# One encoder block on one core: late tokens' output projections on whole units, and expert-row fetches placed by when their slots come free

## The chip, the cores and the metric

The kernel runs on one core of a Trainium2 chip. The core has five engines with queues of their own: PE (TensorE, with its weight loads as PEld), DVE (VectorE), ACT (ScalarE), POOL (GpSimd) and SP (SyncE, which here only issues DMAs), and 16 DMA engines. The metric is the device time of one execution in microseconds. Before the change three runs took 2066.88, 2083.95 and 2086.36 us, so the median is 2083.95.

## The reference

One layer over 512 tokens of 1024 features, in fp32:

```python
h = rms_norm(x)
aq, ak, av, rq, rk, rv, rg, ga, gr = split(h @ w_in)
y_att = sliding_window_gqa(aq, ak, av, sinks) @ w_o_att      # 8 heads, 2 kv heads, own and previous chunk of 64
y_ret = (silu(rg) * group_norm(retention(rq, rk, rv))) @ w_o_ret   # 4 heads, keys of 256, values of 512
x = x + (sigmoid(ga) * y_att + sigmoid(gr) * y_ret) @ w_out
x = x + peer(rms_norm(x))     # 8 heads; top 16 of 128 x 128 experts by two half keys; gelu(h . down) * gate * up
x = x + sigmoid(rms_norm(x) @ w_ple_gate) * (p @ w_ple_proj)
out = rms_norm(x)
```

## The kernel before, in words

**Tokens.** The first 128 tokens (the early tile) go through the mixers first, up to their top-k lists; then the other 384 (the late tokens) follow. What is asked here is the late part.

**Weights.** All weights come as units of 128 x 1024 fp32, 512 KB each, through a ring of 8 slots `raw` that SP fills in the order of `late_units()` (line 73). A slot is loaded again once PE has used the unit 8 before (`wait_used`, for value and gate batches after the whole batch of four). In the late part a product with weights is made of three fp32r products: ACT makes the high half of a unit (`upper`, L700), POOL the low half (`lower`, L650), and PE runs hi x hi, hi x lo and lo x hi (`mm3`, L1184 to L1186) in `columns` (L1198; a key is one tile of 128 outputs) and `tokens` (L1214; four units together, tokens as outputs). The input is split too, for the norm and also for `b_hi`, `b_lo` (the gated retention outputs, `transposed_upper` on ACT and `transposed_lower` on DVE, L2080, and the attention outputs, L949 and L2174) and for the merged mixer output (`merged_lower`, L2205). ACT makes high halves up to four units ahead of the output that it next works on (`run_ahead`).

**Order in the late part.** For each retention head i: rq (2 units), rk (2), rv (4), `wor` of the head before (4 units, 8 keys), rg (4); group norm of the head at its end. Then ak, av, gr, `wor` of the last head, more gr; eight aq and four filler units, in whose loop attention is staged over DVE, ACT and PE (scores of head h in iteration h+2, transposes in h+3, values, `att_out` L1510, in h+4); then `woa` with ga between; `out`; 16 pq units with the norm; then 128 `dn` (expert down) and 128 `up` units. Of the down units every other one is split (even ones), the odd ones are multiplied whole with `h_whole`, which POOL makes at L673 when it reaches the first.

**Expert rows of the early tile.** The first tile's 128 experts per token are fetched one row per token at a time: POOL issues an indirect DMA of 128 x 1024 fp32 (512 KB) into one of 8 slots (`fetch`, L653 to L664), and DVE uses it (`row`, L1757; L1772 for down, L1780 for up). Rows 0 to 127 are of the early tile's down weights, 128 to 255 of its up weights, 256 to 383 the last tile's down weights, the rest its up weights, in the up stage. `ROWS_AFTER`, `AQ_ROWS`, `LIST_ROWS`, `SUM_ROWS` and `QUAD_ROWS` say between which of DVE's other work its rows stand; `FETCH` says behind which unit in POOL's order a fetch stands. A fetch of row r waits for row r-8 to be used. POOL works strictly in this order: for each unit its low half, if it has one, then its fetches.

**The lists.** From pq on DVE makes the top-k lists of the late tokens (`best`, 16 lists, with sums of pairs behind each odd one), five rows beside each: one row after each of its five steps. ACT copies key scores into 12 buffers; the copies of 12 to 15 wait for lists 0 to 3 (`s12_free`, L986), and the high half of unit 252 (`run_ahead(DN0 + LEAD - 1)`, L1008) stands behind the copy of key scores 14, which waits for list 2. The first gelu of the down stage stands behind the copy of 15. Units are numbered over all: pq is 232 to 247, dn begins at 248, up at 376. After 70 down units PE waits for the selected keys, which DVE gives after all lists.

## Time and profile before

| | before |
|---|---|
| runs | 2066.88, 2083.95, 2086.36 us |
| profiled execution | 2086.6 us, its span 2084.8 us |
| mean granted PE clock | 0.957 |
| busy in the span | PE 91%, PEld 72%, DVE 60%, ACT 27%, POOL 47% |
| chain that ended last | PE 55%, DVE 14%, DMA 12%, POOL 10%, issue 5%, ACT 3% |
| moved by DMA | 622.96 MB, mean 299 GB/s |

The share of an engine is its busy time over the span. The chain is followed back from the last instruction, at each step to what released it. An engine's timeline lists its instructions with, in brackets, the idle time before one and who ended it. Stages lie one after the other in time: early tile to 268 us, retention to 682, attention to 811, woa and out to 912, pq and lists to 1244, gates and down units to 1568, up units to 2011, the rest to the end.

### The profile page before, as it was taken

The numbers are of one execution on the slowest core, as the hardware profiler recorded it, in microseconds if no ns is written. First come the engines' busy times: TensorE is split into PE (matmuls) and PEld (weight loads), VectorE is DVE, ScalarE is ACT, GpSimd is POOL, SyncE is SP. The second block draws the span as 40 slices with busy tenths as digits, with TensorE's granted clock in tenths as the row PEclk, the third lists the DMA queues.
The fourth block names the chain that finished last, engine by engine and source line by source line (L and its number), as shares of the span: only waits on it lengthen the run. The fifth ranks groups of instructions, "written<-read, shape, count | busy, mean of one in ns | idle before, by whom it ended". The sixth has DMA issues, their size and how long they took to land.

```text
span 2084.8 us, 25711 instructions
## 1 busy us (share of the span) xinstructions
PE 1886.8 (91%) x9521; PEld 1503.3 (72%) x9521; DVE 1247.7 (60%) x2421; ACT 553.4 (27%) x1024; POOL 971.3 (47%) x726
## 2 busy tenths in 40 slices
PE   7999999989898669989899979999639999999998
PEld 7499987877778558989899878889634444444467
DVE  3120366756557664678779997775664455444556
ACT  1120132322233234333222227774100000000043
POOL 0000066676768426758876635456662222233222
PEclk9999999999999889999999989999868999999999
DMA  8777736777787545779999968999999999999941
GB/s 318 283 264 288 257 122 223 257 253 259 247 309 265 174 160 177 259 241 333 354 414 395 347 199 291 380 378 399 410 404 362 389 390 391 393 392 391 397 147 41
DMA packets 211687, 622.96 MB, mean 299 GB/s; under 512 B 19456, under 2 KB 60544, under 8 KB 210432
## 3 DMA queue, kind: packets, MB, share of 16 engines
q1 hardware_dynamic: 77392, 274.06, 35.5%
q0 software_dynamic: 73728, 268.47, 34.8%
q10 hardware_dynamic: 60464, 79.11, 11.1%
q8 instruction: 58, 0.95, 0.2%
q14 instruction: 45, 0.37, 0.1%
HBM read 580.67 MB, written 37.75 MB: 297 GB/s over the span
## 4 chain that ended last, share of the span: by engine, by line
PE 55%; DVE 14%; DMA 12%; POOL 10%; issue 5%; ACT 3%; SPq 0%; ACTq 0%; POOLq 0%; DVEq 0%
PE bank L1672 21%; DMA slots<-peer_down,scr 8%; PE bank L1184 6%; PE bank L1186 6%; PE bank L1185 6%; PE bank L1269 6%; POOL w_lo L650 5%; POOL slots L664 5%; DVE slots L1772 2%; PE bank L1290 2%; PE bank L1600 2%; DVE bank L1780 2%; DMA raw<-weights 2%; DMA slots<-peer_up,scr 1%; PE bank L1344 1%
## 5 line engine op out<-in xcount | busy, mean ns | idle before, releaser
L650 POOL TENSOR_TENSOR w_lo<-raw,w_hi 128x1024 fp32r<-128x1024 f32 x198 | 472.3, 2392 | 637.9 <-ACT w_hi L700 635.8
L1184 PE MATMUL bank<-hb,w_hi 128*128 128x384 f32 (+2 forms) x1320 | 450.2, 341 | 55.0 <-POOL w_lo L650 28.0
L1672 PE MATMUL bank<-raw,scr 128*128 128x512 f32 x1024 | 442.6, 595 | 28.1 <-DVE scr L2378 28.1
L1185 PE MATMUL bank<-hb,w_hi 128*128 128x384 f32 (+2 forms) x1320 | 431.5, 327 | 0.0
L1186 PE MATMUL bank<-hb,w_lo 128*128 128x384 f32 (+2 forms) x1320 | 431.2, 327 | 0.0
L1772 DVE SCALAR_TENSOR_TENSOR slots<-slots,bank 128x1024 f32<-128x1024 f32 x256 | 308.8, 1218 | 173.0 <-DMA slots<-peer_down,scr 165.4
L664 POOL DMA_INDIRECT slots<-peer_up,scr x256 | 244.2, 954 | 343.8 <-DVE bank L1780 291.6
L1672 PEld LDWEIGHTS bank<-raw,scr 128*128 128x128 f32 x1024 | 195.6, 191 | 274.7 <-issue 274.7
L700 ACT ACTIVATE w_hi<-raw 128x1024 fp32r<-128x1024 f32 x198 | 205.3, 1053 | 559.1 <-DMA raw<-weights 548.8
L1780 DVE SCALAR_TENSOR_TENSOR bank<-slots,scr,bank 128x1024 f32<-128x1024 f32 x254 | 325.7, 1282 | 33.7 <-DMA slots<-peer_up,scr 29.6
L1184 PEld LDWEIGHTS bank<-hb,w_hi 128*128 128x128 f32 x1320 | 262.4, 199 | 66.1 <-POOL w_lo L650 29.5
L664 POOL DMA_INDIRECT slots<-peer_down,scr x256 | 243.3, 950 | 108.4 <-issue 79.7
L1185 PEld LDWEIGHTS bank<-hb,w_hi 128*128 128x128 f32 x1320 | 262.4, 199 | 4.8 <-issue 1.0
L1186 PEld LDWEIGHTS bank<-hb,w_lo 128*128 128x128 f32 x1320 | 261.4, 198 | 2.9
L1600 PE MATMUL bank<-x_all,raw 128*128 128x256 f32 x1024 | 235.4, 380 | 1.0 <-ACT scr L1021 1.0
L1600 PEld LDWEIGHTS bank<-x_all,raw 128*128 128x128 f32 x1024 | 189.7, 191 | 24.0 <-issue 1.2
L2378 DVE TENSOR_TENSOR scr<-scr 128x256 f32<-128x256 f32 x128 | 54.7, 429 | 221.0 <-PE bank L1672 218.2
L1021 ACT ACTIVATE scr<-bank 128x256 f32<-128x256 f32 x128 | 48.4, 379 | 231.1 <-PE bank L1186 136.8
L1184 PE MATMUL bank<-w_hi,hb 128*128 128x512 f32 (+1 forms) x216 | 86.0, 398 | 19.3 <-POOL w_lo L650 15.7
L1269 PE MATMUL bank<-slots,raw 128*128 128x128 f32 x672 | 78.8, 279 | 10.8 <-DVE slots L1851 10.8
L1046 ACT ACTIVATE scr<-hb,scr 128x128 f32<-128x128 f32 x256 | 81.2, 391 | 23.2 <-DVE hb L2352 22.8
L1269 PEld LDWEIGHTS bank<-slots,raw 128*128 128x128 f32 x672 | 78.1, 196 | 11.8 <-issue 11.7
(304 smaller groups left out, 1861.6 us busy)
## 6 DMA issues: line engine op xcount, KB each, us to landing
raw<-weights SPq DMA_DIRECT2D x514, 512.0 KB, 6.7
act_scratch<-scr ACTq DMA_DIRECT2D x64, 256.0 KB
gate_scratch<-scr ACTq DMA_DIRECT2D x8, 2048.0 KB, 8.8
scr<-gate_scratch ACTq DMA_DIRECT2D x32, 512.0 KB, 16.5
scr<-act_scratch ACTq DMA_DIRECT2D x32, 512.0 KB, 20.5
slots<-peer_down,scr POOLq DMA_INDIRECT x256, 7.9
slots<-peer_up,scr POOLq DMA_INDIRECT x256, 7.9
x_all<-x_scratch ACTq DMA_DIRECT2D x1, 2048.0 KB, 17.4
```

Source lines behind the costliest of these rows:

```text
L650: nc.gpsimd.tensor_tensor(w_lo[:, s, :], raw[:, s, :], w_hi[:, s, :].bitcast(F32), ALU.subtract).then_inc(lo_done, 1)
L664: pool.indirect_dma_start(slots[:, r % R_SLOTS, :], None, up_d if part % 2 else down_d, bass.IndirectOffsetOnAxis(ap=ids[:, n:n + 1], axis ...
L700: nc.scalar.activation(w_hi[:, u_mod, :], raw[:, u_mod, :], ACT.Copy).then_inc(hi_done, 1)
L1046: ins = nc.scalar.activation(gated[q % 4][:, x, :], onehot(q, x, 1).bitcast(F32), ACT.Copy, scale=gates_s[:, t + x:t + x + 1])
L1184: nc.tensor.matmul(out, a_hi, c_hi, start=first, stop=False)
L1185: nc.tensor.matmul(out, a_hi, c_lo, start=False, stop=False)
L1186: return nc.tensor.matmul(out, a_lo, c_hi, start=False, stop=last)
L1269: ins = nc.tensor.matmul(out, raw[:, u % RING, k * P:k * P + P], rhs[:, k, :], start=k == 0, stop=k == KT - 1)
L1600: ins = nc.tensor.matmul(bank[:, c % 2, 0:T], raw[:, s, P * k:P * k + P], h_whole[:, k, :], start=k == 0, stop=k == KT - 1)
L1672: ins = nc.tensor.matmul(bank[:, b, :], wgt[:, c % 4, a], raw[:, s, 512 * n:512 * n + 512], start=first, stop=last)
L1772: ins = stt(out=u, in0=u, scalar=1.0, in1=row_bank, op0=ALU.mult, op1=ALU.mult, accum_out=dots[:, n:n + 1])
L1780: ins = stt(out=row_bank, in0=u, scalar=a, in1=row_bank, op0=ALU.mult, op1=ALU.add)
```

## The change

Part one: the 32 `wor`, `woa` and `out` units of the late tokens are no longer split. PE multiplies the raw unit with the unsplit input in plain fp32 (`whole_columns`), one product for three. So their high and low halves go, and with them the splits of the inputs: `transposed_lower`, the b_lo of attention and `merged_lower` on DVE, the copies of the merged output on ACT; ACT writes the unsplit inputs into `yT` and `att`, and `out` reads `yacc`.

Part two: in the attention loop the scaling of the probabilities (3 instructions a head) goes from DVE to ACT, behind ACT's copy of the transposes. The gelu of the early tile's dots goes from the attention loop to behind ga 4.

Part three: rows in the late mixers are spread otherwise. In the attention loop 20 rows in 7 iterations (3 each, the last 2) become 11 rows in 11; the 3, 6, 3 and 6 rows at the values and gates of heads 2 and 3 become 3, 4, 4 and 4, the 3, 3, 0 and 6 of head 1 become 3, 3, 3 and 4; woa 0 to 5 have 4 for 3; all in all 167 for 168 before the lists, and 89 for 88 in them. 66 rows stay behind the gates in both.

Part four: `FETCH` comes from a plan (`fetch_plan`) that steps through DVE's, PE's and POOL's work with costs in microseconds and puts each fetch behind the last unit whose low half begins before the slot comes free. From the code before and after, these are the numbers of fetches placed behind a unit, and in all up to it:

| units | before | after |
|---|---|---|
| 140, 141, 142 (head 1's values but the last) | 2, 4, 0 | 0, 0, 2 |
| 156, 157, 158 (head 2's) | 2, 2, 2 | 1, 1, 9 |
| 172, 173, 174 (head 3's) | 2, 2, 2 | 7, 0, 4 |
| 164, 165, 166 (gates of head 2's turn) | 2, 2, 2 | 2, 2, 2 |
| 180, 181, 182 (gates of head 3's turn) | 2, 2, 2 | 6, 3, 1 |
| up to 240 (pq 8) | 172 | 174 |
| up to 245 (pq 13) | 186 | 182 |
| up to 248 (dn 0) | 192 | 182 |
| up to 249 (dn 1) | 194 | 190 |
| up to 253 (dn 5) | 201 | 197 |
| up to 258 (dn 10) | 208 | 197 |
| up to 259 (dn 11) | 209 | 205 |
| up to 268 (dn 20) | 220 | 211 |
| up to 269 (dn 21) | 221 | 219 |
| up to 278, 279 (dn 30, 31) | 232, 233 | 225, 229 |
| up to 374 (dn 126), and at 375 | 371, 13 more | 354, 30 more |

The diff, cut to its core:

```diff
+def is_split(u):
+
+    return u >= NE and UNITS[u][0] not in ("wor", "woa", "out", "up") and (u < DN0 or u >= PP0 or (u - DN0) % 2 == 0)
+
+
+SPLITS = list(itertools.accumulate(int(is_split(_u)) for _u in range(NU)))
...
+    return SPLITS[u]
...
-ROWS_AFTER = {("rg", 0, LT - 1): 2,
-              ("rv", 1, 0): 3, ("rv", 1, 2): 3, ("rg", 1, LT - 1): 6}
+ROWS_AFTER = {("rg", 0, LT - 1): 2}
 for _i in range(1, RH):
-    for _k in (("rq", 2 * _i), ("rq", 2 * _i + 1), ("rk", 2 * _i), ("rk", 2 * _i + 1)):
-        ROWS_AFTER[_k] = 1
+    for _k, _n in ((("rq", 2 * _i), 1), (("rq", 2 * _i + 1), 1), (("rk", 2 * _i), 1), (("rk", 2 * _i + 1), 1 + (_i > 1)),
+                   (("rv", _i, 0), 3), (("rv", _i, 2), 3 + (_i > 1)), (("rg", _i, 0), 3 + (_i > 1)), (("rg", _i, LT - 1), 4)):
+        ROWS_AFTER[_k] = _n
     for _m in range(KT):
         ROWS_AFTER[("wor", _i - 1, _m)] = 1
-    if _i > 1:
-        ROWS_AFTER[("rv", _i, 0)], ROWS_AFTER[("rv", _i, 2)] = 3, 6
-        ROWS_AFTER[("rg", _i, 0)], ROWS_AFTER[("rg", _i, LT - 1)] = 3, 6
 for _k in (("ak", 0), ("ak", 1), ("gr", 0)):
-    ROWS_AFTER[_k] = 2
+    ROWS_AFTER[_k] = 3
 for _m in range(KT):
     ROWS_AFTER[("wor", RH - 1, _m)] = 1
+for _m in range(2, KT - 2):
+    ROWS_AFTER[("gr", _m)] = 2
 for _m in range(KT):
-    ROWS_AFTER[("woa", _m)] = 3 if _m + 2 < KT else 1
+    ROWS_AFTER[("woa", _m)] = 4 if _m + 2 < KT else 2
     ROWS_AFTER[("out", _m)] = 1 + _m % 2
 for _m in range(RAW_Q):
     ROWS_AFTER[("pq", _m)] = 2
-for _m in range(2, KT - 2):
-    ROWS_AFTER[("gr", _m)] = 2
-_left = NPAIR - sum(ROWS_AFTER.get(_k, 0) for _k in OUT if OUT[_k] < OUT[("aq", 0)])
-AQ_ROWS = {_i: min(3, max(0, _left - 3 * (_i - 1))) for _i in range(1, AH)}
-assert sum(AQ_ROWS.values()) == _left, _left
+AQ_ROWS = {_i: 1 for _i in range(1, AH + 4)}
+_n = sum(ROWS_AFTER.get(_k, 0) for _k in OUT if OUT[_k] < OUT[("woa", 0)]) + sum(AQ_ROWS.values())
+assert _n <= NPAIR, _n
+GELU_AT = next(_m for _m in range(KT) if _n + sum(ROWS_AFTER[("woa", _x)] for _x in range(_m + 1)) >= NPAIR)
...
+COST = {"wor": 5.3, "woa": 5.3, "out": 5.3, "aq": 6.8, "dn": 3.9}
+DVE_COST = {"rq": 1.2, "rk": 2.3, "wor": 0.6, "ak": 2.4, "gr": 0.8, "aq": 5.6, "woa": 1.2, "out": 2.2, "pq": 0.8}
+POOL_COST, FETCH_COST, ROW_COST, LANDING, SEARCH = 2.42, 1.07, 1.31, 8.0, 10.3
+DONE_AT = dict(zip(range(NE, UP0), itertools.accumulate(COST.get(UNITS[_u][0], 4.2) for _u in range(NE, UP0))))
...
+def row_events():
     for k in OUT:
+        if k == ("pq", RAW_Q):
+            break
+        u, less, extra = LAST_UNIT[k], 0.0, 0.0
         if k[0] in ("rv", "rg"):
+            less = 4.2 * 4 * (LT - 1 - k[2]) / LT
+        elif k[0] == "wor":
+            less = 2.6 * (1 - k[2] % 2)
+        if k[0] == "rv":
+            u, less = UNIT[("rk", 2 * k[1] + 1)], 0.0
+            extra = 25.0 if k == ("rv", 1, LT - 1) else 0.0
+        elif k[0] == "rg":
+            extra = (12.0 if k[1] == 1 else 3.0) if k[2] == 0 else 6.0 if k[2] == LT - 1 else 0.0
+        if k in FILLERS or k[0] == "aq":
+            yield u, less, 5.6, AQ_ROWS.get(k[1] if k[0] == "aq" else AH + FILLERS.index(k), 0), u + 3
+        elif k[0] == "rg" and k[2] == LT - 1:
+            yield u, less, 0.0, ROWS_AFTER.get(k, 0), u
+            yield u, 0.0, extra, 0, u
+        else:
+            yield u, less, DVE_COST.get(k[0], 0.0) + extra, ROWS_AFTER.get(k, 0), u + 3
+    last = UNIT[("pq", RAW_Q - 1)]
     for m in range(2 * PH):
+        yield last, 0.0, SEARCH, LIST_ROWS[m] + SUM_ROWS[m], last + 6 + 4 * m if m < 4 else DN0 + STEP * FIRST_Z + LEAD
+    at = DN0 + STEP * FIRST_Z
+    yield at, 0.0, 2.0, DOTS_EXP, at + LEAD + 4
+    yield at + SELECT_AT, 0.0, 2.0, DOTS_SELECT, at + LEAD + 6
     for j, quads in enumerate(QUAD_ROWS):
+        for q in range(4 * STEP // 2):
+            u = at + STEP * (j + 1) + q // 2
+            yield u, 0.0, 1.25, quads.count(q), u + 3
+    yield UP0 - 1, 999.0, 0.0, NLAST, UP0 - 1
...
+def fetch_plan():
+    used, fetch, pool, unit, at, behind = [], {}, 0.0, NE, 0.0, NE
+    first = DONE_AT[UNIT[("rg", 1)]]
+    for u, less, cost, rows, by in row_events():
+        at = max(at, DONE_AT[u] - less) + cost
+        for _ in range(rows):
+            free = max(first, used[-R_SLOTS] + ROW_COST + 0.5) if len(used) >= R_SLOTS else first
+            while unit < UP0:
+                ready = DONE_AT.get(unit - RING, 0.0) + 9.0 if unit < DN0 else DONE_AT[unit - LEAD] + 1.2
+                if is_split(unit):
+                    if max(pool, ready) >= free:
+                        break
+                    pool = max(pool, ready) + POOL_COST
+                unit += 1
+            pool = max(pool, free) + FETCH_COST
+            behind = max(behind, min(unit - 1, by, UP0 - 1))
+            fetch.setdefault(behind, []).append(len(used))
+            at = max(at, pool + LANDING)
+            used.append(at)
+            at += ROW_COST
+    assert len(used) == 3 * NPAIR, len(used)
+    return fetch
+FETCH = fetch_plan()
...
-ROW_USED, NLAST = row_uses()
-FETCH_LAG, FETCH_FIRST = 7, UNIT[("rg", 0)] + 6
-FETCH = {}
-_at = FETCH_FIRST
-for _r in range(3 * NPAIR):
-    if _r >= R_SLOTS:
-        _at = max(_at, ROW_USED[_r - R_SLOTS] + FETCH_LAG)
-    while len(FETCH.get(_at, ())) >= (2 if _r < R_SLOTS else 4):
-        _at += 1
-    FETCH.setdefault(min(_at, UP0 - 1), []).append(_r)
...
+        yT, att = part3(b_plain, 0, 4, L), part3(b_plain, 0, AH, L)
...
-                    nc.scalar.activation(b_hi[:, c, :], late(6 + c % 2), ACT.Copy).then_inc(b_hi_ready, 1)
+                    nc.scalar.activation(yT[:, c, :], late(6 + c % 2), ACT.Copy).then_inc(b_ready, 1)
...
-                    nc.scalar.activation(b_hi[:, h, :], late(7), ACT.Copy).then_inc(b_hi_ready, 1)
+                    nc.scalar.activation(att[:, h, :], late(7), ACT.Copy).then_inc(b_ready, 1)
...
-                if i == AH + 1:
+                if 0 <= i - 2 < AH:
+                    h = i - 2
+                    sc.wait_ge(rden_ready, h + 1)
+                    for t in range(LT):
+                        nc.scalar.activation(a_s[:, h % 2, t, :], a_s[:, h % 2, t, :], ACT.Copy,
+                                             scale=rden[:, t:t + 1]).then_inc(p_ready, 1)
+            for m in range(1, KT):
+                to_tile(("ga", m), ACT.Sigmoid)
+                if m == min(GELU_AT + 2, KT - 1):
                     sc.wait_ge(row_done, NPAIR)
                     nc.scalar.activation(dots, dots, ACT.Gelu_apprx_tanh).then_inc(dots_gelu, 1)
-            for m in range(1, KT):
-                to_tile(("ga", m), ACT.Sigmoid)
 
             for m in range(KT):
-                sc.wait_ge(yacc_ready, RH * KT + m + 1)
-                nc.scalar.activation(h_hi[:, m, :], merged(m), ACT.Copy).then_inc(h_hi_ready, 1)
                 run_ahead(UNIT[("ga", KT - 1)] + 4 + min(m, 4))
...
+            def whole_columns(key, rhs, kt=KT, u=None, at=0, width=P, tiles=None):
+
+                u = UNIT[key] if u is None else u
+                wait_landed(pe, u)
+                bank_free(key)
+                for k in range(kt):
+                    if tiles is not None:
+                        pe.wait_ge(tiles[0], tiles[1] + k + 1)
+                    o = k * width + at
+                    ins = nc.tensor.matmul(proj_bank(key), raw[:, u % RING, o:o + P], rhs[:, k, :],
+                                           start=k == 0, stop=k == kt - 1)
                 ins.then_inc(proj_done, 1)
 
...
-                    columns(("wor", i, m), b_hi, b_lo, kt=4, u=UNIT[("wor", 4 * i + m // 2)],
-                            at=P * (m % 2), width=2 * P)
+                    whole_columns(("wor", i, m), yT, kt=4, u=UNIT[("wor", 4 * i + m // 2)],
+                                  at=P * (m % 2), width=2 * P)
...
-                columns(("woa", m), b_hi, b_lo, tiles=(b_ready, 4 * RH) if m == 0 else None)
+                whole_columns(("woa", m), att, tiles=(b_ready, 4 * RH) if m == 0 else None)
...
-                columns(("out", m), h_hi, h_lo, tiles=(h_ready, KT) if m == 0 else None)
+                whole_columns(("out", m), yacc, tiles=(yacc_ready, RH * KT) if m == 0 else None)
...
-                    ve.wait_ge(h_hi_ready, (KT * (r + 1) if r else 0) + k + 1)
+                    ve.wait_ge(h_hi_ready, KT * r + k + 1)
...
-            def transposed_lower(i, cs):
-                for c in cs:
-                    ve.wait_ge(b_hi_ready, 4 * i + c + 1)
-                    mark(tt(b_lo[:, c, :], late(6 + c % 2), b_hi[:, c, :].bitcast(F32), ALU.subtract), b_ready)
...
-                if 0 <= i - 4 < AH:
-                    h = i - 4
-                    ve.wait_ge(b_hi_ready, 4 * RH + h + 1)
-                    mark(tt(b_lo[:, h, :], late(7), b_hi[:, h, :].bitcast(F32), ALU.subtract), b_ready)
...
-                    step(nc.vector.reciprocal(rden[:, 0:LT], rden[:, 0:LT]))
-                    for t in range(LT):
-                        ts(a_s[:, h % 2, t, :], a_s[:, h % 2, t, :], rden[:, t:t + 1], None, ALU.mult).then_inc(p_ready, 1)
+                    mark(nc.vector.reciprocal(rden[:, 0:LT], rden[:, 0:LT]), rden_ready)
                 rows(AQ_ROWS.get(i, 0))
 
-            def merged_lower(ns):
-                for n in ns:
-                    ve.wait_ge(h_hi_ready, KT + n + 1)
-                    mark(tt(h_lo[:, n, :], merged(n), h_hi[:, n, :].bitcast(F32), ALU.subtract), h_ready)
-
             for m in range(KT):
-                if m == KT - 2:
-                    merged_lower((0, 1))
                 z = next_tile()
                 key = ("woa", m)
                 wait_output(ve, key)
                 step(tt(prod_p, proj_bank(key), z, ALU.mult))
                 ve.sem_inc(tile_free, 1)
                 ve.sem_inc(free_of(key), 1)
-                mark(tt(merged(m), yacc[:, m, :], prod_p, ALU.add), yacc_ready)
-                if m == KT - 2:
-                    merged_lower(range(2, KT - 2))
+                mark(tt(yacc[:, m, :], yacc[:, m, :], prod_p, ALU.add), yacc_ready)
                 rows_after(key)
...
-            merged_lower((KT - 2, KT - 1))
```

## Rows read from the trace of the kernel before

**Rows 1.** The page: busy time by engine; DMA share by 40 slices, in tenths.

```profile
PE 1886.8 (91%) x9521; PEld 1503.3 (72%) x9521; DVE 1247.7 (60%) x2421; ACT 553.4 (27%) x1024; POOL 971.3 (47%) x726
...
DMA  8777736777787545779999968999999999999941
```

**Rows 2.** Busy by stage: PE, PEld, DVE, ACT, POOL, then PE clock, DMA share, GB/s.

```profile
682.00:811.00 129.00, 87.40 (x453) 80.81 (x453) 72.92 (x147) 48.48 (x101) 48.44 (x35) 0.84 0.48 158
...
1003.00:1244.00 241.00, 220.79 (x1385) 205.89 (x1386) 220.37 (x656) 66.80 (x110) 153.44 (x110) 0.97 0.92 351
...
1450.00:1568.00 118.00, 64.91 (x342) 58.71 (x340) 75.14 (x125) 12.66 (x25) 74.66 (x69) 0.78 1.03 408
```

**Rows 3.** The same view, over fifty microseconds of woa and ga units.

```profile
812.00:862.00 50.00, 50.00 (x290) 50.00 (x290) 32.06 (x34) 17.98 (x25) 41.93 (x28) 1.00 0.78 280
```

**Rows 4.** The chain that ended last: start, us, what (plain products).

```profile
1014.33 3.54 PE bank L1600 x16
...
1568.38 442.58 PE bank L1672 x1024
```

**Rows 5.** The page, costliest groups: the low and the high halves.

```profile
L650 POOL TENSOR_TENSOR w_lo<-raw,w_hi 128x1024 fp32r<-128x1024 f32 x198 | 472.3, 2392 | 637.9 <-ACT w_hi L700 635.8
...
L700 ACT ACTIVATE w_hi<-raw 128x1024 fp32r<-128x1024 f32 x198 | 205.3, 1053 | 559.1 <-DMA raw<-weights 548.8
```

**Rows 6.** PE's timeline: start, us, then idle before in brackets.

```profile
345.96 0.79 PE L1184 MATMUL bank<-w_hi,hb 128*128 128x512 f32 x1 [5.10 <-POOL w_lo L650]
...
431.52 0.80 PE L1184 MATMUL bank<-w_hi,hb 128*128 128x512 f32 x1 [5.04 <-POOL w_lo L650]
...
511.37 0.41 PE L1184 MATMUL bank<-hb,w_hi 128*128 128x384 f32 x1 [3.49 <-DVEq L2055]
...
607.98 0.36 PE L1184 MATMUL bank<-w_hi,hb 128*128 128x256 f32 x1 [3.60 <-ACTq L734]
```

**Rows 7.** POOL's timeline ahead of the second head's values.

```profile
414.78 2.42 POOL L650 TENSOR_TENSOR w_lo<-raw,w_hi 128x1024 fp32r<-128x1024 f32 x1 [10.56 <-ACT w_hi L700]
...
419.57 2.40 POOL L650 TENSOR_TENSOR w_lo<-raw,w_hi 128x1024 fp32r<-128x1024 f32 x1
```

**Rows 8.** The chain, a row of the third head's expert values.

```profile
494.43 8.09 DMA slots<-peer_down,scr
```

**Rows 9.** PE's timeline in the attention loop: att_out of three iterations.

```profile
707.13 2.93 PE L1510 MATMUL bank<-scr 128*128 128x128 f32 x12 [6.34 <-ACT scr L963]
...
781.36 2.12 PE L1510 MATMUL bank<-scr 128*128 128x128 f32 x12 [2.60 <-ACT scr L963]
...
794.01 1.60 PE L1510 MATMUL bank<-scr 128*128 128x128 f32 x12 [2.60 <-ACT scr L963]
```

**Rows 10.** DVE's timeline in the same loop: the softmax begins.

```profile
776.28 0.96 DVE L2180 SCALAR_TENSOR_TENSOR scr<-bank,scr 128x768 f32<-128x768 f32 x1
```

**Rows 11.** PE's timeline: the first out unit.

```profile
872.63 0.69 PE L1184 MATMUL bank<-hb,w_hi 128*128 128x384 f32 x1 [4.82 <-DVE hb L2208]
```

**Rows 12.** The chain in the list stage: two landings and h_whole.

```profile
942.98 4.68 DMA slots<-peer_up,scr
...
988.35 5.59 POOL x_all L673 x8
...
998.91 7.47 DMA slots<-peer_up,scr
```

**Rows 13.** DVE's timeline: an expert row beside the third list.

```profile
981.60 1.27 DVE L1780 SCALAR_TENSOR_TENSOR bank<-slots,scr,bank 128x1024 f32<-128x1024 f32 x1
```

**Rows 14.** ACT's timeline: a high half, and the last key scores' copy.

```profile
995.64 1.05 ACT L700 ACTIVATE w_hi<-raw 128x1024 fp32r<-128x1024 f32 x1
...
1006.53 0.49 ACT L987 ACTIVATE scr<-bank 128x384 f32<-128x384 f32 x1 [9.84 <-DVEq L2305]
```

**Rows 15.** PE's timeline: third down unit, and the end of the lists.

```profile
1008.86 0.55 PE L1184 MATMUL bank<-hb,w_hi 128*128 128x256 f32 x1 [5.96 <-ACT scr L1021]
...
1243.92 0.66 PE L1649 MATMUL bank<-small,scr 128*128 128x128 f32 x2 [11.97 <-DVE scr L2336]
```

46 lines of the change are left out of this document (8 added, 38 removed).

## The prediction

> **What bounds the kernel now.** I read the page's busy shares and slices first, then the busy time by stage, then the chain, and last the timelines of PE, POOL, DVE and ACT around PE's gaps. PE is busy 91% of the span and the DMA engines are full over the last half [rows 1]. By stage [rows 2] the reader is to see three kinds. The attention loop (682 to 811 us) keeps PE busy 87 of 129 us at a granted clock of 0.84: a chain of waits between engines. The stage of the late top-k lists (1003 to 1244 us) has PE and DVE busy 221 and 220 of 241 us: two engines that must meet at its end. The end of the expert-down stage (1450 to 1568 us) has the DMA share at 1.03: it is limited by bytes. In the retention stage PE is nearly full, and its few gaps have names [rows 6]: POOL's low halves, DVE, ACT.
>
> **The unit prices.** A projection unit of three fp32r products per tile runs at 290 records in 50 us [rows 3], so 24 take 4.14 us. A plain product is two records: with 256 columns a unit of 16 records takes 3.54 us with its tail, 0.216 us a record (16 in 3.46), and with 512 columns 442.58 us over 1024 records is 0.432 [rows 4]. Both are 0.844 ns a column and record, so 384 columns cost 0.324 us a record and 5.19 us a unit. Each of the 32 changed units (16 wor, 8 woa, 8 out) costs PE 1.05 us more: **+33.5 us**, if all of it is on the path. Sides of that price: it can't be under the 256-column record (3.46 us, -0.7 a unit) nor over the 512-column one (6.9 us, +2.8). I take 5.19, since both neighbours give one price a column.
> The Trainium skill (FP8 and Floating Point Precision, TensorE Precision Notes) says that true fp32 takes 4 passes through the array, which speaks against this change. As an estimate from that page, 4 against 3 passes would make 5.52 us a unit and +44 us. The rows give 5.19 against 4.14, a ratio of 1.25, so the sum stays with them.
>
> What is taken away: 32 low halves on POOL at 2.39 us and 32 high halves on ACT at 1.05 [rows 5], and DVE's and ACT's splits of the inputs. POOL and ACT mostly wait there anyhow, so this counts only where PE waits for them. SP issues the same loads in the same order and its waits don't change; the whole units need only their landing.
>
> **Retention, 268 to 682 us.** POOL's order counts: four low halves of a value batch start when ACT is through with the group norm (414.78), and every fetch between them costs what the step from 414.78 to 419.57 shows: 4.79 us for one half and two fetches, 1.19 a fetch [rows 7]. Before the fourth half stand 6 fetches in each head, and PE waits 5.10 and 5.04 us for heads 1 and 2 [rows 6]. By the new plan they are 2, 11 and 11 for heads 1, 2 and 3.
> - Head 1: four fewer, 4.8 us; PE's wait goes. Its wor units cost +4.3 (16.9 to 21.2, DVE keeps up). Net -0.5.
> - Head 2: 414.78 + 4 x 2.4 + 11 x 1.19 = 437.5 in place of 431.5: **+6.1**. wor grows to 21.2 but loses 2.4 us of waits for DVE, with half a microsecond of late rows: +1.8.
> - Head 3: the gap of 3.49 us at 511.37 [rows 6] comes from the last of nine rows, which landed at 502.5 [rows 8]; with eight, fetched without a break, it lands before y is ready and the gap goes. POOL's queue is 11 fetches again, counted from an earlier start (505.5 + 22.7 against 527.8): +0.2 together. Ahead of the third gate batch stand 10 fetches for 6: 6.6 + 9.6 + 11.9 = 28.1 us after the values against the 24.4 of before: +3.8.
> - Last head: the gap of 3.60 us at 607.98 [rows 6] goes in the same way, and DVE no longer stands behind ACT's copies of the transposes: -6.5 with the dearer wor in it.
> Sum **+4.9**.
>
> **Attention, 682 to 811 us.** Without rows one iteration takes 794.01 - 781.36 = 12.65 us [rows 9]: att_out 1.6, the rest of the projection 2.6, scores 1.0, then softmax on DVE and exps and copy on ACT from 776.28 to 781.36, 5.1 us [rows 10]. That is 10.4; the other 2.2 are DVE's b_lo ahead of the softmax, which the change removes, and half clock. With three rows an iteration takes 14.5 to 16.4. One row (1.3 us) fits beside PE's 5 us, and the scaling of p, now 3 ACT copies of about 0.5, comes behind the copy that PE waits for. I take 11.2 for all: from 703 (707.13 less two rows and the scaling) six iterations end at 770, not 794.01, and the last step loses DVE's wait of 1.8 us too. **-22**; sides -10 (rows still land late) and -30 (10.4 each and at full clock).
>
> **woa, ga and out, 811 to 912 us.** 16 units, +16.8. Four rows, two adds and their waits are 6.5 us on DVE beside 9.3 of PE, and 4 fetches and a half are 7.2 on POOL: covered. The moved gelu holds DVE for some 4 us inside that slack; without it woa would wait. out starts on yacc directly: the gap of 4.82 us at 872.63 [rows 11] goes, since its first seven tiles (4.5 us) cover the last add, and with it 3.4 us of half clock. **+8.6**.
>
> **Lists, 912 to 1244 us.** No instruction changes here, only the places of the fetches. The plan of before has 194 fetches out by the second down unit and 209 by the twelfth; the new one holds back to 182 through the first down unit, then sends 8 at unit 249, 7 at 253, 8 at 259, 8 at 269. It gives a list 10.3 us ahead of its rows, in whole blocks, where DVE interleaves them. So what is late:
> - Row 182. POOL reaches unit 249 after the low half of 247 (978), h_whole 5.59 us [rows 12] and the half of 248: 986. Landing takes 4.7 to 7.5 us [rows 12]; row 182 is there at 992.5. DVE wanted it at about 984: it ran row 182's equal at 981.60 [rows 13].
> - List 2 ends at 1001.6. ACT copies key scores only once its slot is free, so the high half of unit 252 goes from 995.64 [rows 14] to 1002.6, and fetch 190, behind it, to 1006. Row 190 at 1014, row 191 at 1016, list 3 at 1018. ACT's copy waited 9.84 us for that list before, until 1006.53 [rows 14]; now until 1018. Behind it stand the first gelu and PE's third down unit, which waited until 1008.86 [rows 15]: now 1020.
> - Fetches 197 to 204 come behind unit 258's half, which ACT makes after the fifth down unit: 1037, landed 1044, 25 us late. Then DVE catches up (2 us a row against 2.4), until fetch 225 at unit 279: rows 225 and 226 at 1108 to 1111, where DVE stood at 1092.
> From there on rows come in time in both. DVE's lag of **+18.5** is passed on whole, since PE waits for DVE at the end (11.97 us at 1243.92 [rows 15]) and is itself only some 14 late. Sides: 0 if DVE's pace is the plan's, +28 if the bursts' lag is half as much again.
> By the Trainium skill (DMA: Bandwidth & Descriptors, Anatomy of one DMA), a DMA takes about 2 us and its bytes over 436 GB/s, 3.2 us a row as an estimate; the sum would then have 14 here. The rows show 4.7 to 7.5 under load, and stand.
>
> **The rest.** Gates and down: both plans keep 7 fetches per 4 units; 0, +-4. Tail: 30 fetches behind the last unit in place of 13, but DMA is full there (1.03) and bytes don't change: PE's waits shrink, the up stage starts when the last row is in. 0, +-6. The up stage is untouched.
>
> Sum: +4.9 - 22 + 8.6 + 18.5 = +10 on the profiled execution's 2086.6 us, so 2096.6. The median shown is 2.65 lower: **2094**.
>
> **Rivals.**
> 1. *The fetches keep DVE fed* (the lists cost nothing). For it: the old plan keeps POOL waiting for slots late in the stage, so part of its lead is of no use. Against it: cumulative counts fall below what DVE had already used at the same unit. Time: 2094 - 18.5 = 2075.
> 2. *Faster by over 1%*: the lists keep pace, and POOL works the 11 fetches in its idle 10.6 us [rows 7] rather than behind the halves, which gives back 12 us: 2063, and 2055 with the attention loop at 10.4. Against it: POOL's order is fixed, and these fetches stand behind the first half.
> 3. *Slower by over 1%*: the burst at the tail. 30 rows remain when the last unit is done; from the point where PE's last down units finish more than 8 rows' time early, only eight slots are in flight and DMA is no longer full; at 17 further rows and 1.2 to 1.5 us each that is +20 to +25 on top: 2116. For it: the up stage begins 28 us after PE is free even now. Against it: 8 rows of 0.5 MB are 10 us of DMA work.
> 4. *The bill for PE is paid in full*, gains elsewhere stay hidden: +33.5 less the gaps 4.8, 3.5, 3.6 and 4.8 alone is +17 before the lists. It needs attention to gain nothing; it ends near 2116 too.
>
> **Chances.** The forecast 0.47 (own range 2083 to 2107), rival 1 0.22, rival 2 0.16, rivals 3 and 4 together 0.15. A measurement of this kernel can tell about 1% from no change (2063 and 2105 here). Faster: 0.16 and a tail of rival 1, 0.21. Slower: 0.15 and the top of the forecast's range, 0.23. Same 0.56. The range 2057 to 2114 leaves out half of rival 2 and more than half of 3 and 4, some 0.18.
>
> **What would show it.** Waits of PE for POOL of some 11 us before heads 2 and 3's values and none for head 1; att_out every 11 us; no gap before out; PE's wait for ACT behind the second down unit of 17 us, not 6; DVE waits for rows of 8 to 15 us near there; the wait at the end of the lists of 12 us or more. Wrong if that stage's DVE waits are below 20 us in all, or if the down stage's last waits differ by over 10 us.

## The result, and the profile after

Three runs took 2102.00, 2104.91 and 2106.91 us: median 2104.91, a ratio to before of 1.011 with the interval 1.006 to 1.016. The profiled execution took 2106.91 us, its span 2105.1. The forecast of 2094 is 11 us too low, inside its range. Medians are over all executions (three of after, five to twelve of each kernel below); one of e8 (6694 us) and two of e9 (3287 and 5508 us) were slow ones, which the ratios leave out and without which their medians are 2073.04 and 2096.97. The difference of the two spans is 20.3 us, and it lies in these stretches:

| stretch (start in before and after, us) | before | after | difference | predicted |
|---|---|---|---|---|
| up to the first attention scores (687.3, 685.0) | | | -2.3 | +4.9 |
| from there to the seventh att_out of eight (794.0, 768.6) | 106.7 | 83.6 | -23.1 | -22 |
| to the second down unit (999.3, 982.5) | 205.3 | 213.9 | +8.6 | +8.6 |
| to the selection of keys (1243.9, 1254.6) | 244.6 | 272.1 | +27.5 | +18.5 |
| to the first up unit (1568.4, 1589.4) | 324.5 | 334.8 | +10.3 | 0 |
| to the end (2084.8, 2105.1) | 516.4 | 515.7 | -0.7 | 0 |

The page of after, its busy times and its DMA shares in 40 slices, against [rows 1]:

```profile
PE 1897.4 (90%) x9265; PEld 1449.7 (69%) x9265; DVE 1223.2 (58%) x2365; ACT 528.4 (25%) x1009; POOL 892.2 (42%) x694
...
DMA  8778746667689339777999868989999999999941
```

PE is busy 11 us longer, and 20 us of span are added: about half of the loss is waiting. By stage the busy time grows by 5.1 us in retention and 13.4 in woa and out, where 16 whole units each were to cost 16.8, and falls by 6.1 in attention; the granted clock is higher in all three (0.97 for 0.96, 1.00 for 0.97, 0.89 for 0.83). POOL and ACT have 79 and 25 us less to do, and it helps little.

The seventh att_out is where the prediction's count of the attention loop ends. Counted by whole stages (first woa unit at 806.3 and 783.0, first pq unit at 911.5 and 896.3) the differences are -20.9 for attention, +8.0 for woa and out and -1.5 for pq.

Busy time of after in the three stretches of [rows 2], shifted to where they now lie; columns as there (PE, PEld, DVE, ACT, POOL, PE's granted clock, DMA share, GB/s):

```profile
680.00:786.00 106.00, 79.56 (x434) 72.79 (x435) 52.68 (x96) 53.87 (x120) 28.41 (x18) 0.89 0.35 113
986.00:1255.00 269.00, 226.53 (x1388) 209.12 (x1387) 233.69 (x680) 66.67 (x112) 152.30 (x111) 0.93 0.87 321
1471.00:1589.00 118.00, 58.85 (x336) 53.96 (x334) 77.51 (x127) 12.53 (x25) 76.22 (x73) 0.75 1.03 408
```

The lists' stretch is 28 us longer, and its DMA share falls from 0.92 to 0.87. The end of the down stage still moves 408 GB/s: it is full in both.

PE's timeline of after, its long waits (start, duration, then in brackets the idle time before and who ended it), against [rows 6], [rows 9] and [rows 15]:

```profile
435.98 0.79 PE L1217 MATMUL bank<-w_hi,hb 128*128 128x512 f32 x1 [11.46 <-POOL w_lo L679]
532.39 0.79 PE L1217 MATMUL bank<-w_hi,hb 128*128 128x512 f32 x1 [11.22 <-POOL w_lo L679]
756.40 1.92 PE L1556 MATMUL bank<-scr 128*128 128x128 f32 x12 [2.78 <-ACT scr L992]
768.62 2.93 PE L1556 MATMUL bank<-scr 128*128 128x128 f32 x12 [2.76 <-ACT scr L992]
999.10 0.55 PE L1217 MATMUL bank<-hb,w_hi 128*128 128x256 f32 x1 [12.83 <-ACT scr L1054]
1254.60 0.66 PE L1695 MATMUL bank<-small,scr 128*128 128x128 f32 x2 [15.02 <-DVE scr L2357]
1374.86 0.38 PE L1662 MATMUL bank<-scr,hb 128*128 128x128 f32 x1 [4.49 <-ACT scr L1079]
1589.39 11.01 PE L1718 MATMUL bank<-raw,scr 128*128 128x512 f32 x20 [46.42 <-issue]
```

Before the values of head 1 the wait is 0.22 us now, before those of heads 2 and 3 one of 11 us each. att_out comes every 10.65 us (713.81, 724.44, 735.10, 745.76, 756.40), but the step before these is 13.4 us, the one behind them 12.2 and the last 10.5 (779.10). The wait ahead of `out` (4.82 us in [rows 11]) is gone. The wait before the up units grows from 28.09 to 46.42 us.

DVE's timeline of after: its two longest waits for rows in the lists, one very long instruction, and a wait in the gates:

```profile
975.51 1.29 DVE L1826 SCALAR_TENSOR_TENSOR bank<-slots,scr,bank 128x1024 f32<-128x1024 f32 x1 [6.25 <-DMA slots<-peer_up,scr]
...
1021.25 1.29 DVE L1826 SCALAR_TENSOR_TENSOR bank<-slots,scr,bank 128x1024 f32<-128x1024 f32 x1 [12.67 <-issue]
...
1184.09 6.56 DVE L2281 TENSOR_SCALAR scr<-scr 128x96 uint32<-128x96 uint32 x1
...
1371.13 1.22 DVE L1818 SCALAR_TENSOR_TENSOR slots<-slots,bank 128x1024 f32<-128x1024 f32 x1 [7.35 <-DMA slots<-peer_down,scr]
```

The first two waits are for rows 182 and 197, which the prediction named; for row 190, the third that it named, DVE waits 1.03 us. The third line is an instruction of 0.2 us that takes 6.56; nothing in the prediction answers to it.

These figures add up to the lists' loss. In the 90 us before the second down unit DVE waits 22.2 us for rows where it waited 9.1, from there to the selection 30.3 where it waited 21.2, and the long instruction is 6.3 more: 28.5 us, and the stretch is 27.5 longer.

### The profile page after: what moved, and what is told of

It reads as the page before. It is cut to its first block, busy times and chain, and to the rows that moved or that the text cites. A ratio compares the mean times of both kernels' runs of the same rounds, so it can differ in the third digit from the quotient of the medians.

```text
span 2105.1 us, 25084 instructions
## 1 busy us (share of the span) xinstructions
PE 1897.4 (90%) x9265; PEld 1449.7 (69%) x9265; DVE 1223.2 (58%) x2365; ACT 528.4 (25%) x1009; POOL 892.2 (42%) x694
## 4 chain that ended last, share of the span: by engine, by line
PE 59%; DVE 13%; POOL 10%; DMA 9%; issue 6%; ACT 3%; SPq 0%; ACTq 0%; POOLq 0%; DVEq 0%
PE bank L1718 21%; PE bank L1256 7%; PE bank L1315 6%; PE bank L1217 5%; POOL w_lo L679 5%; PE bank L1219 5%; PE bank L1218 5%; POOL slots L693 4%; DMA slots<-peer_down,scr 3%; DMA slots<-peer_up,scr 2%; DVE bank L1826 2%; DMA raw<-weights 2%; PE bank L1336 2%; DVE slots L1818 2%; PE bank L1534 1%
## 5 line engine op out<-in xcount | busy, mean ns | idle before, releaser
L679 POOL TENSOR_TENSOR w_lo<-raw,w_hi 128x1024 fp32r<-128x1024 f32 x166 | 394.2, 2383 | 682.8 <-ACT w_hi L729 681.6
L1217 PE MATMUL bank<-hb,w_hi 128*128 128x256 f32 (+2 forms) x1064 | 361.5, 340 | 41.5 <-POOL w_lo L679 26.6
L1218 PE MATMUL bank<-hb,w_hi 128*128 128x256 f32 (+2 forms) x1064 | 341.7, 321 | 0.0
L1219 PE MATMUL bank<-hb,w_lo 128*128 128x256 f32 (+2 forms) x1064 | 341.2, 321 | 0.0
L729 ACT ACTIVATE w_hi<-raw 128x1024 fp32r<-128x1024 f32 x166 | 173.1, 1053 | 565.8 <-DMA raw<-weights 556.8
L1217 PEld LDWEIGHTS bank<-hb,w_hi 128*128 128x128 f32 x1064 | 211.5, 199 | 51.7 <-issue 28.4
L1218 PEld LDWEIGHTS bank<-hb,w_hi 128*128 128x128 f32 x1064 | 211.5, 199 | 5.7 <-issue 1.0
L1219 PEld LDWEIGHTS bank<-hb,w_lo 128*128 128x128 f32 x1064 | 210.3, 198 | 2.8
L1256 PE MATMUL bank<-hb_plain,raw 128*128 128x384 f32 x384 | 125.9, 486 | 1.0 <-DVEq L2136 1.0
L1256 PEld LDWEIGHTS bank<-hb_plain,raw 128*128 128x128 f32 x384 | 72.5, 190 | 49.3 <-issue 1.6
L1315 PE MATMUL bank<-slots,raw 128*128 128x128 f32 x672 | 79.5, 281 | 11.4 <-DVE slots L1897 11.4
```

Source lines behind the costliest of these rows:

```text
L679: nc.gpsimd.tensor_tensor(w_lo[:, s, :], raw[:, s, :], w_hi[:, s, :].bitcast(F32), ALU.subtract).then_inc(lo_done, 1)
L729: nc.scalar.activation(w_hi[:, u_mod, :], raw[:, u_mod, :], ACT.Copy).then_inc(hi_done, 1)
L1217: nc.tensor.matmul(out, a_hi, c_hi, start=first, stop=False)
L1218: nc.tensor.matmul(out, a_hi, c_lo, start=False, stop=False)
L1219: return nc.tensor.matmul(out, a_lo, c_hi, start=False, stop=last)
L1256: ins = nc.tensor.matmul(proj_bank(key), raw[:, u % RING, o:o + P], rhs[:, k, :], start=k == 0, stop=k == kt - 1)
```

## The experiments

Each of the kernels below but two (e5 and e8) is the changed kernel with other places for some fetches. `N[r]` is the unit behind which the changed kernel fetches row r, `O[r]` the unit that the rule of before gives for the new row uses, `U[r]` the one used. The times by stage are from each kernel's profiled execution: start of the first scores, the second down unit, the selection and the first up unit. Each ratio is against executions of before taken beside that kernel's (medians 2083.86 for e1 to e4, 2084.34 for e5 to e8, 2083.25 for e9 to e12). Up to the second down unit profiled executions of kernels that are alike there (after, e2, e3, e6, e9, e10, e11) differ by up to 8 us, so stretches are compared behind it, not arrivals.

| run | median us | ratio to before, 95% | scores | down | selection | up | down to selection | selection to up |
|---|---|---|---|---|---|---|---|---|
| before | 2083.95 | | 687.3 | 999.3 | 1243.9 | 1568.4 | 244.6 | 324.5 |
| after | 2104.91 | 1.006 to 1.016 | 685.0 | 982.5 | 1254.6 | 1589.4 | 272.1 | 334.8 |
| e1 old plan | 2052.19 | 0.983 to 0.989 | 667.5 | 962.3 | 1207.6 | 1530.9 | 245.3 | 323.3 |
| e2 old lists | 2086.16 | 0.999 to 1.002 | 685.9 | 980.6 | 1232.4 | 1570.3 | 251.8 | 337.9 |
| e3 old tail | 2106.14 | 1.009 to 1.015 | 682.9 | 974.4 | 1248.7 | 1582.3 | 274.3 | 333.6 |
| e4 values | 2076.31 | 0.996 to 0.999 | 660.0 | 957.0 | 1230.9 | 1564.4 | 273.9 | 333.5 |
| e5 units only | 2080.92 | 0.997 to 1.001 | 678.5 | 997.6 | 1243.2 | 1569.2 | 245.6 | 326.0 |
| e6 old gates | 2086.86 | 1.000 to 1.005 | 681.2 | 975.4 | 1240.7 | 1566.2 | 265.3 | 325.5 |
| e7 values, old rest | 2040.79 | 0.976 to 0.982 | 658.3 | 955.8 | 1201.0 | 1525.8 | 245.2 | 324.8 |
| e8 rows only | 2073.44 | 0.993 to 0.997 | 673.3 | 983.7 | 1229.5 | 1555.6 | 245.8 | 326.1 |
| e9 rows 256-263 | 2097.77 | 1.004 to 1.010 | 687.7 | 981.3 | 1245.7 | 1578.7 | 264.4 | 333.0 |
| e10 rows 264-280 | 2112.24 | 1.009 to 1.017 | 687.9 | 982.0 | 1254.7 | 1595.5 | 272.7 | 340.8 |
| e11 rows 197-204 | 2102.52 | 1.006 to 1.014 | 683.1 | 977.8 | 1246.4 | 1581.4 | 268.6 | 335.1 |
| e12 burst back | 2051.11 | 0.980 to 0.987 | 659.6 | 954.2 | 1205.8 | 1534.3 | 251.6 | 328.5 |

### The plan, undone as a whole and by stages

**e1**, the whole plan:

```diff
-U = N
+U = O
```

> The changed kernel (whole units, new row uses), with all 384 fetches placed by the rule of the kernel before, applied to the new row uses. Theory A (the plan is what costs: the 11 us waits of PE before the values of heads 2 and 3, +26 us from the first query unit to the top-k selection, and bytes not moved in that time that the end of the down stage owes): the waits before the values fall to some 5 us, the stretch from the first query unit to the selection falls from 358 us to some 335, and the wait before the up stage from 46 us to under 35; time 2065 to 2078, faster than the kernel before. Theory B (the dearer whole units and the spread rows bring the lag of VectorE, whatever the plan): within 5 us of the changed kernel, 2100 to 2110.

2052.19 us: 53 us less than the changed kernel, more than theory A had. Theory B has fallen. Parts one to three together gain 32 us; part four loses 53.

**e2**, the lists: `U[167:256] = O[167:256]`.

> The changed kernel, with only the fetches of rows 167 to 255 (those of the late lists' stage) behind the units where the rule of before puts them. Theory A (fetches held back through the first down unit starve VectorE): its waits for rows in that stage go from 30 us to under 12, the selection comes 18 to 26 us earlier, and the wait before the up stage shrinks too, since more bytes have moved by then: 2070 to 2087. Theory B (the lag comes from what VectorE brings along, or from POOL's own load): selection within 6 us of the changed kernel's, 2098 to 2108.

-18.7 us. The stretch to the selection is 20.3 us shorter, and the wait of 12.67 us is gone: DVE's longest wait left there is

```profile
981.89 1.29 DVE L1873 SCALAR_TENSOR_TENSOR bank<-slots,scr,bank 128x1024 f32<-128x1024 f32 x1 [4.95 <-DMA slots<-peer_up,scr]
```

Theory A, but not all of it: DVE's waits for rows behind the second down unit fall from 30.3 to 22.4 us, near before's 21.2, and not under 12; and the 7 us that are left over before's stretch, and the 45.65 us before the up units, did not go.

**e3**, the tail: `U[318:] = O[318:]`.

> The changed kernel, with only the fetches from row 318 on (the last 66 of the down stage) where the rule of before puts them. Theory A (the longer wait of 46 against 28 us before the up stage is owed for bytes that were not moved in the list stage, and the place of the last fetches is indifferent since the DMA engines are full there): within 4 us of the changed kernel, 2101 to 2109. Theory B (the burst of 30 fetches behind the last unit leaves the DMA engines short): the wait falls by 8 to 15 us and the time to 2090 to 2097.

2106.14 us, theory A. PE's wait before the up units falls from 46.42 to 28.76 us and its last down unit ends 16 us later, counted from the selection, so that the stretch from the selection to the up units stays (333.6 for 334.8). While PE waits there DVE uses a row of 0.5 MB every 1.28 us, at a DMA share of 1.03, in either order. The wait's length told only when PE had run out of down units.

**e4**, the values of heads 2 and 3:

```diff
+for _r in range(28, 39):
+    U[_r] = 155 if _r < 35 else 159
+for _r in range(56, 67):
+    U[_r] = 171 if _r < 63 else 175
```

> The changed kernel, with rows 28 to 34 and 56 to 62 fetched ahead of the low half of the first value unit of heads 2 and 3, in the time in which POOL waits for the group norm, and rows 35 to 38 and 63 to 66 behind that of the last one. Theory A (POOL's fixed order makes PE's two waits of 11.5 and 11.2 us): both waits fall below 3 us, the first query unit starts 15 to 22 us earlier and the whole passes that on, 2083 to 2092. Theory B (the time is taken back, since VectorE or the DMA engines set the pace of the stages behind): the first query unit is earlier, but the selection or the up stage is less than half of that earlier, 2095 to 2105.

-28.6 us in the medians, -25 us at the first up unit of the profiled executions: theory A, and more than its range. POOL's timeline of after, its part before the values of head 3:

```profile
509.48 2.41 POOL L679 TENSOR_TENSOR w_lo<-raw,w_hi 128x1024 fp32r<-128x1024 f32 x1 [12.85 <-ACT w_hi L729]
512.04 0.96 POOL L693 DMA_INDIRECT slots<-peer_down,scr  x1
...
519.52 0.94 POOL L693 DMA_INDIRECT slots<-peer_down,scr  x1 [0.30 <-issue]
520.48 4.65 POOL L679 TENSOR_TENSOR w_lo<-raw,w_hi 128x1024 fp32r<-128x1024 f32 x2
...
529.98 2.36 POOL L679 TENSOR_TENSOR w_lo<-raw,w_hi 128x1024 fp32r<-128x1024 f32 x1
```

POOL idles 12.85 us, then makes the first half, and only then issues the seven fetches behind it, with four more ahead of the last half. In e4 the same fetches fill most of the idle time (4.38 us are left), and the four halves follow each other:

```profile
493.09 0.94 POOL L744 DMA_INDIRECT slots<-peer_down,scr  x1 [0.30 <-issue]
498.41 9.50 POOL L730 TENSOR_TENSOR w_lo<-raw,w_hi 128x1024 fp32r<-128x1024 f32 x4 [4.38 <-ACT w_hi L780]
```

Both waits of PE are gone, and nothing behind takes the gain back.

**e6**, rows 256 to 317: `U[256:318] = O[256:318]`.

> The changed kernel, with only the fetches of rows 256 to 317 (behind the second half of the down units, up to the tail) where the rule of before puts them. Theory A (up to the up stage the changed kernel takes 334 us from the selection on, the one with all fetches by the old rule 323, and undoing the last 66 fetches left it at 334: so the 10 us lie in the fetches between): 2093 to 2099, the wait before the up stage under 38 us. Theory B (the 10 us are bytes owed from the list stage, wherever the fetches behind it stand): 2102 to 2108.

-18 us, more than either theory. The stretch behind the selection is 9.3 us shorter, as theory A has it, though the wait before the up units stays at 46.00 us where it expected under 38; and the stretch before the selection is 6.8 us shorter too. That was the first sign of a cost in the lists that late rows did not explain.

### The long instruction

In e6 DVE waits for rows in the lists about as long as in after (28.2 and 29.3 us from row 197 to the selection), but the instruction of 6.56 us is 0.2. POOL's timeline of after at that place:

```profile
1182.57 0.95 POOL L693 DMA_INDIRECT slots<-peer_down,scr  x1 [0.79 <-issue]
1183.54 7.04 POOL L679 TENSOR_TENSOR w_lo<-raw,w_hi 128x1024 fp32r<-128x1024 f32 x3
```

Eight fetches stand behind unit 301. Their issue keeps POOL from 1172.22 to 1183.52 us, 1.25 us each and up to 0.7 more for the last three, whose slots come late. The halves that come due in that time are then made back to back, 1183.54 to 1190.57, and DVE's instruction of 1184.09 ends at 1190.65. **e9** takes only this burst apart (`U[256:264] = O[256:264]`), **e12** adds only it to the fastest version.

> The changed kernel with only the fetches of rows 256 to 263 (eight behind one unit) spread behind five units as by the rule of before. In the trace of the changed kernel POOL works three low halves back to back behind that burst (1183.54 to 1190.57 us), and one small instruction of VectorE, 0.2 us elsewhere, takes 6.56 us from 1184.09. Theory A (VectorE is locked out while POOL's halves follow each other, and the burst makes them do so): that instruction takes under 1 us, the selection comes 5 to 8 us earlier counted from the first down unit, 2096 to 2101. Theory B (the stretch hides behind a wait that comes anyway): 2102 to 2108.

> The fastest version so far (values' rows moved ahead, old rule from row 167 on, 2041 us) with only the burst of rows 256 to 263 behind one unit put back. Theory A (the burst alone makes POOL's halves follow each other and locks VectorE out): an instruction of VectorE stretched to some 6 us, the selection 5 to 8 us later, 2046 to 2049. Theory B (it needs the late rows before it, by which POOL waits for slots): within 3 us of 2041.

Both came out by theory A, e12 with 2051.11 us somewhat above its range: e9 is 7.1 us faster than after and its stretch to the selection 7.7 shorter; e12 is 10.3 us slower than e7, its stretch 6.4 longer, and another 3.7 us, which are not traced, come behind the selection. DVE's instruction in e9, then DVE and POOL in e12:

```profile
1181.49 0.21 DVE L2328 TENSOR_SCALAR scr<-scr 128x96 uint32<-128x96 uint32 x1
```

```profile
1135.27 6.52 DVE L2333 TENSOR_SCALAR scr<-scr 128x96 uint32<-128x96 uint32 x1
...
1134.72 7.00 POOL L731 TENSOR_TENSOR w_lo<-raw,w_hi 128x1024 fp32r<-128x1024 f32 x3
```

The reader sees one small instruction that starts half a microsecond behind POOL's first half and ends with the third. The Trainium skill (SBUF — State Buffer, Who interferes with whom) says that DVE and GpSimd share one pair of ports, held as an exclusive lock for a whole instruction; that DVE waits agrees with it, and here it waited through three instructions, not one. What e9 and e12 show is that the bunch of halves makes the long instruction; that the lock is what holds it is taken from the page.

The same thing stands in after's retention stage, where DVE's and POOL's timelines have

```profile
584.23 7.54 DVE L2080 TENSOR_TENSOR scr<-scr,misc 128x128 f32<-128x128 f32 x1
...
582.17 9.44 POOL L679 TENSOR_TENSOR w_lo<-raw,w_hi 128x1024 fp32r<-128x1024 f32 x4
```

Both end at 591.6 to 591.8 us, so here DVE waits through what is left of four halves. It is in all ten profiles that keep the plan's places there (7.2 to 7.6 us) and in none of before, e1, e5 and e8. PE has no wait near it, so it costs nothing that the profile shows.

### Parts of the lists and of the gates alone

**e11**: `U[197:205] = O[197:205]`.

> The changed kernel with only the fetches of rows 197 to 204 behind the units of the rule of before (down units 4 to 8 and not all behind the eleventh). Theory A (this burst makes VectorE's longest wait for rows in the lists, 12.7 us at 1021 us, and the lag is passed on to the selection): that wait falls below 4 us and the selection comes 9 to 13 us earlier, 2092 to 2096. Theory B (the bursts before and behind it, rows 182 to 196 and 205 to 263, hold VectorE up by as much as it is ahead): selection less than 5 us earlier, 2100 to 2106.

-2.4 us, and the stretch 3.5 us shorter: theory B (the intervals of the two ratios overlap, so the 2.4 us are not clear of noise). The rows of the burst are issued 14 us earlier, counted from the second down unit, and DVE meets a wait of 8.24 us at 1029.15 for the next one, behind down unit 15. So this burst does not carry the lag alone; the next one takes over.

**e10**: `U[264:281] = O[264:281]`.

> The changed kernel with only the fetches of rows 264 to 280 where the rule of before puts them: four units later at the start (row 264 behind down unit 73, not 69, where POOL waits 29 us for its slot with three low halves behind it). Theory A (POOL stuck there delays the first gate units, and that is the 9 us that the stretch from the selection to the last down unit is longer): 2095 to 2099, the stretch 280 us and not 288. Theory B (the 9 us come from rows 281 to 317, which the new plan puts one unit later here and there, so that they land just behind VectorE's turn): 2102 to 2108, the stretch unchanged.

Theory A has fallen, and 2112 us is above the range of theory B too: 7 us slower than after, and the stretch behind the selection 6 us longer. POOL's wait for the slot of row 264 falls from 29.17 to 15.01 us and nothing is gained by it. PE's waits in that stretch are as long as in after; what grows is its busy time, 260.7 us for 254.3 with the same 1678 records, at a granted clock of 0.90 to 0.93 for 0.97 to 1.00 between 1300 and 1450 us. So what e6 gains in this stretch (9.3 us) lies in rows 281 to 317, by elimination, and its size there is uncertain by some 6 us; this range was not run alone. The traces give a mechanism. There many rows move by one unit, and where that is from an odd unit to the even one behind it, the fetch comes to stand behind that unit's low half, which waits for ACT. Rows 295 and 296 are such a pair (`O` down unit 93, `N` 94; the first row moved in this way is 292). POOL in after:

```profile
1359.82 2.40 POOL L679 TENSOR_TENSOR w_lo<-raw,w_hi 128x1024 fp32r<-128x1024 f32 x1 [6.81 <-ACT w_hi L729]
1362.38 0.95 POOL L693 DMA_INDIRECT slots<-peer_down,scr  x1 [0.15 <-issue]
```

It is issued at 1362.38, DVE's wait for a row ends at 1371.13, ACT's copy starts at 1373.53 and PE's wait of 4.49 us ends at 1374.86 (the lines above). In the whole stretch PE waits 20.6 us for such copies, and 10.3 in e6. That the one-unit moves are the cause is read from this chain, not shown by a run.

### The other three parts

**e5** is the kernel before with the whole units, **e8** with the new row uses, both with the rule of before for the fetches; e1 has both.

```diff
 # e5: the changed kernel with ROWS_AFTER and AQ_ROWS of before
-AQ_ROWS = {_i: 1 for _i in range(1, AH + 4)}
+AQ_ROWS = {_i: min(3, max(0, _left - 3 * (_i - 1))) for _i in range(1, AH)}
...
+U = O
```

```diff
 # e8: the kernel before with ROWS_AFTER and AQ_ROWS of after
-AQ_ROWS = {_i: min(3, max(0, _left - 3 * (_i - 1))) for _i in range(1, AH)}
+AQ_ROWS = {_i: 1 for _i in range(1, AH + 4)}
...
-                if i == AH + 1:
+                if m == min(GELU_AT + 2, KT - 1):
                     sc.wait_ge(row_done, NPAIR)
```

> The kernel before with the whole units and inputs and the scaling of p on ScalarE, but its own row uses (three rows in most attention iterations) and its own rule for the fetches. Theory A (the units cost PE their 1.05 us each in the stages where it is full, and give back some waits for splits; the attention loop stays long because its rows stay): 32 units +33.5 us, less the waits before and behind them of some 20, less 10 in attention: 2080 to 2092. Theory B (it is the units and the lighter VectorE that make the 32 us gain of the changed kernel with the old rule for fetches): 2052 to 2065.

> The kernel before with its split units, the new row uses (one row in each attention iteration, the other uses spread), the gelu of the early dots moved as this needs, and the rule of before for the fetches. Theory A (the spread rows make the attention loop shorter by 1 to 3 us an iteration, and this alone gains): 2062 to 2074. Theory B (the loop needs both, since VectorE's splits of the head outputs and its scaling stand in it whatever the rows are; the rows put elsewhere cost their time there): 2078 to 2090.

Medians against before's 2084: units -3.4 (the interval includes no change), rows -10.9, both (e1) -32. Theory A in each, and 18 us more than the sum when both are done. The attention loop, from the first scores to the seventh att_out, tells where 14 of them lie: 106.7 us before, 105.6 with the units, 97.5 with the rows, 82.2 with both. att_out in e5 comes every 13.2 to 15.8 us, in e8 mostly every 13.8 and then 12.65, in e1 every 10.66 between a first and a last step of 12.1. The timelines give a reason, which no run isolates. In e8, with one row, DVE is idle for 6.28 us of an iteration, but its b_lo, which waits for ACT, stands ahead of the softmax and its scaling ahead of the transposes. In e1 the chain from PE over the softmax and ACT back to PE has neither.

**e7**, the fastest: the edit of e4 and `U[167:] = O[167:]`.

> The changed kernel with rows 28 to 38 and 56 to 66 fetched as in the run that moved them ahead of the value units, and all fetches from row 167 on by the rule of before. Theory A (the two costs are separate and add: PE has no waits for low halves in the retention stage, and the lists, gates and tail run as with the old rule): 5 us less than with the old rule throughout, which kept waits of 5.0, 2.7 and 3.8 us there: 2043 to 2050. Theory B (with the earlier arrival VectorE and the DMA engines set the pace, and the gain is taken back at the up stage): 2050 to 2060.

2040.79 us, 2 us below the range of theory A, 2.1% below the kernel before (interval 1.8 to 2.4%) and 64 below the changed one. Its first up unit starts 5.1 us before e1's, though the medians differ by 11. The four stages of the plan, undone alone, gave 28.6 (values), 18.7 (lists), 18.0 (rows 256 to 317) and -1.2 us (tail): 64 in all. The costs add, though that they do so to the microsecond is chance, with only three executions of after, 4.9 us apart. Its stretch that answers to the lists' of after:

```profile
958.00:1201.00 243.00, 223.51 (x1391) 208.01 (x1389) 221.26 (x661) 66.89 (x110) 155.84 (x111) 0.96 0.93 351
```

The lists' stretch has the pace of before again (243 us for 241, 351 GB/s for 351).

## Why the prediction was right, and where it was not

The parts were forecast as a gain in attention against a loss in the lists, and so they came. That the sum is only 10 us off is partly luck: retention came out 7 us better than its term, and the lists and the gates together 19 us worse.

**The price of a whole unit** was right: the eight `out` units of after take 849.28 to 890.73 us, 5.18 each at a granted clock of 1.00, and the estimate was 5.19 from records of other widths. The estimate of 5.52 went wrong by its base, not by the four passes of the Trainium skill (FP8 and Floating Point Precision, TensorE Precision Notes): a plain product takes 1.69 ns a column here, four times 0.42, but an fp32r product takes 0.45 and not 0.42 (24 in 4.14 us), so three of them cost more than three quarters of a plain one.

**Retention** was wrong by 7 us (-2.3 for +4.9), though its named waits came as forecast: none before head 1's values, 11.46 and 11.22 before those of heads 2 and 3. The seven profiles that are alike up to there reach the first scores at 681.2 to 687.9 us and the forecast would be 692.2, so this is more than their spread, though before has only one profile. What was sized wrong is the rest. From the values of head 3 (527.8 and 532.4) to the first scores the time falls by 7.0 us where +3.8 and -6.5 were forecast, and between the values of heads 2 and 3 it grows by 0.2 for +2.0. The same shows in e5, which reaches the scores 8.8 us earlier than before with the same row uses and rule: PE's idle time from 268 us to there falls from 38.5 to 20.7 us. These are waits for DVE and ACT, which the sum counted only in part. The two waits themselves were priced by their difference to those of before, +6.1 and +0.2; e4 shows that the two waits are worth 25 to 29 us against a plan that uses POOL's idle time.

**Attention** was right (-23.1 for -22), and so was the cadence (11.4 us in the mean of six steps for 11.2). But its own terms, 794 - 770 and 1.8 for the last step, add up to 26, not 22, and the last step did not shrink: it takes 10.5 us for 8.3, since DVE's wait of 1.78 us became one of 1.19 for ACT and PE enters it at half clock (768.62: 2.93 us for the 1.60 of before). **woa and out** came to +8.0 for +8.6; the +8.6 of the table is this last step and pq's gain besides, so that it is right to the tenth is luck.

**The lists** were right in kind and too small: +27.5 for +18.5. Of the late rows that were named DVE waits 6.25 us for 182 and 12.67 for 197, but only 1.03 for 190; ACT's wait at the third down unit is 12.83 us (17 were forecast), and without the plan's places 20.3 us go, near the 18.5. The missing 7 are the burst behind unit 301 and the lock between POOL and DVE, which no step of the prediction had. The step "Then DVE catches up, until fetch 225 ... From there on rows come in time in both" is true of the rows in the lists, and missed that fetches that are in time can still push POOL's halves together. And the sum followed one row after another where e11 shows that the burst with the longest wait does not carry the lag alone.

**The rest** failed: "Gates and down: both plans keep 7 fetches per 4 units; 0, +-4". The counts are nearly the same, the places in POOL's order are not, and they cost 9.3 of the +10.3 us (e6); the way from the places to the loss is read from one chain. **The tail** was right: its price is nothing (e3), so rival 3 has fallen, although the down stage's last waits differ by 18 us. The prediction had named such a difference as a sign against itself; it was a bad sign to choose, since in a stretch limited by bytes the wait moves with PE's last unit and not with the end.

**Rivals.** Rival 1 (the fetches keep DVE fed) has fallen by e2. Rival 2 needed POOL to work the fetches in its idle time; POOL's order forbade it, as the prediction said, and e4 shows what that was worth. Rival 4 needed attention to gain nothing and has fallen by the -23.1 us there; in e1 the gains cover the 33.5 us of the units and 32 more.

## What to carry to other kernels

In a queue that is worked strictly in order, a fetch costs by what stands behind it: put it into the queue's known idle time, ahead of the work that waits for another engine, and spread bursts, since the work behind them bunches while they are issued. Counts per unit do not tell this; the place relative to the next dependent instruction does. Take work off an engine in a loop completely enough that another path becomes the longer one (units or rows alone gained 1 and 9 us in attention, both 24), and judge a stage limited by bytes by when its last byte lands, not by the wait at its end.
